# A kernel's input turned by products with diagonal matrices of reciprocal roots, instead of scaled and then turned

## The reference, cut to what matters

```python
def rms_norm(x, g):
    xf = x.astype(jnp.float32)
    y = xf * lax.rsqrt(jnp.mean(xf * xf, axis=-1, keepdims=True) + NORM_EPS)
    return (y * g.astype(jnp.float32)).astype(x.dtype)
...
    h = jnp.concatenate([meta, x], axis=1)
...
        u = rms_norm(h, mix_pre_g[l])
        proj = u @ w_in[l]
        hq, hf, hi, hg, cq, ckv, kpe, gates = jnp.split(proj, splits, axis=-1)
```

## Time and profile before

| | |
|---|---|
| median of 3 runs | 906.28 us |
| the profiled execution, its time | 904.64 us |
| its span | 902.8 us |
| TensorE busy with products | 881.4 us (98%) |
| TensorE busy with weight loads | 841.6 us (93%) |
| VectorE busy | 513.3 us (57%) |
| ScalarE busy | 473.4 us (52%) |
| GpSimd busy | 611.3 us (68%) |
| mean granted clock of TensorE | 0.996 |

### The profile page before, as it was taken

How to read it: one execution, slowest core, us unless ns; L and a number is a source line. 1 busy time by engine, 2 the same in 40 slices (tenths; PEclk the granted TensorE clock), 3 DMA queues, 4 the chain that set the end, 5 groups by cost and what they waited for, 6 DMA issues and landing times.

```text
span 902.8 us, 17105 instructions
## 1 busy us (share of the span) xinstructions
PE 881.4 (98%) x6837; PEld 841.6 (93%) x6837; DVE 513.3 (57%) x1108; ACT 473.4 (52%) x924; POOL 611.3 (68%) x349
## 2 busy tenths in 40 slices
PE   8999999999999999999999999999999999999996
PEld 7985999999998998999999999999988999999786
DVE  6404111599837857535431115878965668799464
ACT  5525755633346546544444444445657564456673
POOL 5702655655556987999998898776764877766153
PEclk9999999999999999999999999999999999999998
DMA  9623733343432564455655673654320627544201
GB/s 277 206 64 102 234 117 107 127 140 95 133 102 94 174 229 159 140 188 191 198 160 172 183 218 90 207 158 135 129 94 1 187 61 217 161 140 144 91 1 47
DMA packets 134334, 128.09 MB, mean 142 GB/s; under 512 B 6480, under 2 KB 131792, under 8 KB 134256
## 3 DMA queue, kind: packets, MB, share of 16 engines
q1 hardware_dynamic: 133776, 126.20, 44.8%
q10 hardware_dynamic: 480, 0.79, 0.3%
HBM read 125.80 MB, written 1.05 MB: 140 GB/s over the span
## 4 chain that ended last, share of the span: by engine, by line
PE 88%; DVE 6%; ACT 2%; issue 1%; DMA 1%; POOL 0%; POOLq 0%; DVEq 0%; ACTq 0%
PE PS L615 24%; PE PS L617 23%; PE PS L616 23%; PE PS L843 3%; PE PS L606 2%; PE PS L753 1%; PE PS L986 1%; DVE PS L2067 1%; PE PS L805 1%; PE PS L1046 1%; DMA ring<-in_w_in 1%; PE PS L801 1%; PE PS L802 1%; PE PS L1017 1%; ACT w_hi L1292 1%
## 5 line engine op out<-in xcount | busy, mean ns | idle before, releaser
L1160 POOL TENSOR_TENSOR w_lo<-ring,w_hi 128x1024 fp32r<-128x1024 f32 (+1 forms) x235 | 539.7, 2312 | 250.0 <-ACT w_hi L1292 239.4
L615 PE MATMUL PS<-x_hi,w_hi 128*128 128x256 f32 (+2 forms) x1560 | 458.3, 294 | 4.0 <-DVE x_lo L2021 0.9
L617 PE MATMUL PS<-x_hi,w_lo 128*128 128x256 f32 (+2 forms) x1560 | 443.9, 285 | 0.0
L616 PE MATMUL PS<-x_lo,w_hi 128*128 128x256 f32 (+2 forms) x1560 | 442.9, 284 | 0.0
L615 PEld LDWEIGHTS PS<-x_hi,w_hi 128*128 128x128 f32 (+1 forms) x1560 | 293.6, 188 | 8.9 <-issue 6.4
L616 PEld LDWEIGHTS PS<-x_lo,w_hi 128*128 128x128 f32 (+1 forms) x1560 | 293.1, 188 | 1.4 <-issue 0.2
L617 PEld LDWEIGHTS PS<-x_hi,w_lo 128*128 128x128 f32 (+1 forms) x1560 | 293.3, 188 | 0.0
L1292 ACT ACTIVATE w_hi<-ring 128x1024 fp32r<-128x1024 f32 (+2 forms) x233 | 235.5, 1014 | 78.7 <-PE PS L617 72.3
L2067 DVE SCALAR_TENSOR_TENSOR PS<-zoneA,cols,PS 128x256 f32<-128x256 f32 x240 | 98.6, 481 | 0.1
L1275 ACT ACTIVATE zoneA<-PS 128x272 f32<-128x272 f32 (+3 forms) x76 | 29.3, 386 | 107.8 <-PE PS L617 107.8
L1275 ACT ACTIVATE zoneB<-PS 128x256 f32<-128x256 f32 (+4 forms) x115 | 40.9, 378 | 70.7 <-DVE PS L2034 39.8
(11 more groups left out here) (300 smaller groups left out, 1196.0 us busy)
## 6 DMA issues: line engine op xcount, KB each, us to landing
ring<-in_w_in SPq DMA_DIRECT2D x58, 1024.0 KB, 5.4
ring<-in_w_ffn_in SPq DMA_DIRECT2D x22, 1024.0 KB, 5.1
ring<-in_w_out SPq DMA_DIRECT2D x12, 1024.0 KB, 5.0
ring<-in_w_ffn_out SPq DMA_DIRECT2D x16, 704.0 KB, 4.5
ring<-in_w_mla_o SPq DMA_DIRECT2D x4, 1024.0 KB, 5.0
ring<-in_w_hg_o SPq DMA_DIRECT2D x4, 1024.0 KB, 5.0
ring<-in_w_kv_b SPq DMA_DIRECT2D x2, 1024.0 KB, 5.5
ring<-in_w_q_b SPq DMA_DIRECT2D x2, 768.0 KB, 4.9
```

What stands on the lines that cost most here:

```text
L615: mm(out_, hi_w, hi_x, start=start, stop=False)
L616: mm(out_, hi_w, lo_x, start=False, stop=False)
L617: return mm(out_, lo_w, hi_x, start=False, stop=stop)
L1160: sub(lo_w, src, hi_w, ALU.subtract).then_inc(sem("w_lo"), 1)
```

## The change

ScalarE and VectorE no longer scale the input. VectorE multiplies the identity by the column of reciprocals and so makes three small diagonal matrices (16x16, 128x128, 128x128). TensorE no longer turns scaled rows: it multiplies the unscaled rows, as the stationary operand, by the diagonal as the moving one, which scales and turns in one ordinary float32 product. The diagonals come in the order meta rows, first tile, second tile, and TensorE waits for each once, in the first chunk. Waiting for the constants is added on VectorE. The results go to the same places of the same banks, and what follows is as before.

```diff
@@ -443,6 +443,7 @@
         x_nrm = zoneB[:, 4224:4224 + 3 * D].rearrange("p (t d) -> p t d", t=3)
+        x_diag = x_nrm[:, :, 0:P]
@@ -703,15 +704,13 @@
             pe.wait_ge(sem("const_in"), 16)
             for c in range(DC):
-                if c % 4 == 0:
-                    pe.wait_ge(sem(f"x_nrm{c // 4}"), 3)
                 if c >= 4:
                     pe.wait_ge(sem("lo_pre"), c - 3)
                 b = PS[:, 4 + c % 4, :]
-                nc.tensor.transpose(b[:, 0:META], x_nrm[0:META, 2, c * P:(c + 1) * P], ident[0:META, 0:META])
-                for t in range(2):
-                    last = nc.tensor.transpose(b[:, META + t * P:META + (t + 1) * P],
-                                               x_nrm[:, t, c * P:(c + 1) * P], ident)
+                for t, rows, x, at in ((2, META, m_tok[0:META, 0, :], 0), (0, P, x_tok[:, 0, :], META), (1, P, x_tok[:, 1, :], META + P)):
+                    if c == 0:
+                        pe.wait_ge(sem("x_diag"), (2, 3, 1)[t])
+                    last = mm(b[:, at:at + rows], x[:, c * P:(c + 1) * P], x_diag[0:rows, t, 0:rows], start=True, stop=True)
                 last.then_inc(sem("x_turned"), 1)
@@ -1328,10 +1327,6 @@
             af(x_rs, x_sums, ACT.Sqrt, scale=1.0 / D, bias=eps_rms).then_inc(sem("x_std"), 1)
-            act.wait_ge(sem("x_inv"), 1)
-            for half in range(2):
-                cols_ = slice(512 * half, 512 * half + 512)
-                af(x_nrm[:, 0, cols_], x_tok[:, 0, cols_], ACT.Copy, scale=x_rs[:, 0:1]).then_inc(sem(f"x_nrm{half}"), 1)
@@ -1743,11 +1738,10 @@
             dve.wait_ge(sem("m_in"), 16)
-            for half in range(2):
-                cols_ = slice(512 * half, 512 * half + 512)
-                for t, rows, x in ((1, P, x_tok[:, 1, cols_]), (2, META, m_tok[0:META, 0, cols_])):
-                    v.tensor_scalar(x_nrm[0:rows, t, cols_], x, x_rs[0:rows, t:t + 1], None, ALU.mult)\
-                        .then_inc(sem(f"x_nrm{half}"), 1)
+            dve.wait_ge(sem("const_in"), 16)
+            for t, rows in ((2, META), (0, P), (1, P)):
+                v.tensor_scalar(x_diag[0:rows, t, 0:rows], ident[0:rows, 0:rows], x_rs[0:rows, t:t + 1], None, ALU.mult)\
+                    .then_inc(sem("x_diag"), 1)
```

## The result

The kernel after takes 908.72 us, the median of 13 runs (907.61 to 912.11); the kernel before took 905.61 in the same comparison (13 runs, 904.5 to 908.34). The forecast was 907.6.

A forecast was written before the change was run, and what follows sets the result against it. TensorE was taken as the bound, busy 98% of the span: 2.32 us dearer products, less 0.67 for the earlier start and 0.35 for the stall, gave 1.30 later; 906.28 + 1.3 = 907.6 us, range 905.0 to 910.2.

The forecast's parts named there:

- Direction and place: TensorE's turning ahead of the first projection: dearer products make the kernel 1.3 us slower, passed on to the end.
- the mark: First weight load of the projections on TensorE: claimed to move from 14.03 to 15.33, between 14.85 and 17.25.
- The rate: TensorE's turning: a chunk claimed to cost 0.82 us, between 0.76 and 1.06, in place of 0.53.
- The start: TensorE's turning claimed to begin at 8.97, after the last warm-up record, in place of 9.64: 0.67 us earlier.
- The stall of 0.35 ahead of the fifth chunk: TensorE's wait before the fifth turned chunk: claimed to go, as that chunk would start at 12.25, after its release at 12.1.
- VectorE's freed time is worth nothing: VectorE before the first rounding: free at 9.22, but claimed to wait for first weights landing at 10.25, so no gain.
- The diagonals: Three small products on VectorE from 8.65: claimed about 0.2 us each, the third ready at 9.22, before TensorE asks.
- Absorption: Behind the turning: nothing claimed to absorb the shift; GpSimd would lose up to 0.9 us before its third difference.
- The granted clock: TensorE's clock in the turning: read as 1.00 (2.4 GHz) and left there.
- The first (no dearer in place): Rival for the turning: second records disappear in row-change gaps, chunk 0.53, first projection load at 14.03, time 906.3; chance 0.14.
- the third (four turns): Rival for the turning: a product costs four turns, chunk 1.35, 5.5 us later, time 911.8; chance 0.05.
- The second rival: First weights ready at 9.2, so roundings and x_lo move up 1.1 us; with cheap products, time 905.3; chance 0.05.

The follow-up runs named there:

- e3: The kernel after with the 16-row products of two chunks put together, so half as many row changes; 907.16 us, ratio 1.0011 to the kernel before.
- e4: The kernel before with 16-row turns of four and three chunks put together and seven banks for turned chunks; 905.03 us, ratio 0.9985.
- c1_before: The kernel before, unchanged, profiled a second time; span 903.4 us.
- e1: The kernel after, but TensorE turns unscaled rows with the identity; diagonals still made and waited for, no scaling done; 905.54 us, ratio 0.9999.
- e7: The kernel after with 4 unused products in place of 13 ahead of the turning; 913.94 us, ratio 1.0094.
- c2_after: The kernel after, unchanged, profiled a second time; span 907.1 us.

## Why the prediction was right, and where its sizes were off

**Direction and place: right; the size: less than half.** The time grew, within 0.5%, by TensorE's dearer products ahead of the first projection, passed on one to one (the table's last column). But 1.3 us were forecast and 3.1 measured. The 908.72 lies inside 905.0 to 910.2 because the range took in 1.06 us a chunk and the scatter of the runs, and not because the sum was good: the mark was forecast at 15.33, between 14.85 and 17.25, and stood at 16.78 in one profile and at 17.51, outside, in the other.

**The rate: a term too small.** The prediction took 0.82 us a chunk, between 0.76 and 1.06; it is 0.96. The pair was priced at 0.60 and is 0.64. The 16-row product was priced at 0.22, from products with 64-column weights, and is 0.32, the upper end. The term that was mis-sized is the change of rows. I had 0.15 us for the two changes of a chunk, from the pair of turns less 2 × 0.11; e3 measures 0.10 for the one and 0.19 for the other, and 6 × 0.11 + 0.29 gives 0.95. The 0.22 of the 16-row product left only its two records, and nothing for the change behind them. In the turns the missing part sat in the 16-row turn: its 0.16 is not one turn's work, since in e4 four of them stand some 0.06 apart ((0.32 − 0.14) / 3). And the earlier trace rows was no model for the 16-row product: it had half the columns to load, and its records come in pairs that start together (L1083 starts at 691.53 and 691.54, then at 691.59 and 691.60), so four of them took less than two of ours. Eight times 0.14 are 1.1 us of the 1.8 that the forecast was short.

**The start: a step that failed.** The prediction let the turning begin at 8.97, since the last unused product ended there in the one profile, and credited 0.67 us. The runs showed 9.29 and 10.02 for the same kernel, 9.66 in the mean, where the kernel before had 9.64 and 9.73. Nothing was won. In the kernel before the start was at whichever came last, the scalings or the unused products, and c1_before shows that it could already be the latter; when the scalings went, only the unused products were left. The end of these depends on when their rate doubles, and the one profile I had is the one with the earliest doubling of all (the section on the hardware below). For an execution like that one 8.97 may have been right; it was not for the others. In the kernel before, a late start hardly mattered, since the fifth chunk waits for x_lo anyway (marks 14.03 and 13.93). With 9.66 for 8.97 it is 0.7 us, and 1.3 + 1.1 + 0.7 = 3.1.

**The stall of 0.35 ahead of the fifth chunk: right**, it went; e1 shows it back when the rate is the old one.

**VectorE's freed time is worth nothing: right.** It waits for the first weights for 0.80 us after the diagonals, with the rounding at 10.19. In e1, where TensorE is cheap, the mark does not go below 13.83.

**The diagonals: right in effect.** The three take 0.61 from 8.78 on, where I had 0.57 from 8.65 on; without weight, since TensorE came later.

**Absorption: right.** GpSimd's third remainder slipped by 2.5 us (18.60, against 16.12 in the profile before, the third of the five from 11.06 on in the earlier trace rows), with a wait of 2.60 where up to 0.9 was foreseen, and TensorE has no wait for a remainder in the first 66 us of the kernel after.

**The granted clock: the reading was wrong.** I read 1.00 as the upper level. In the turning that was so, but the same column reads 1.00 in e7, where the same six records take 1.68. The column prints 1.00 for any stretch ahead of the trace's first clock record, so at the start of an execution it says nothing; the distance of the records does.

**The rivals.** The first (no dearer in place) and the third (four turns) are refuted by 0.96. The Trainium skill ("TensorE: Matmul & The Clock Gate", section "Terms") gives a factor of four for the turning mode in float32; the trace has 0.11 against 0.225 in streams, and 0.53 against 0.96 a chunk in place, so here it is about two, and the measurement decides. The second rival's condition wasn't met: in the kernel after, in e1 and in e3 VectorE waited for that transfer, 0.80 to 0.91 us, before the first rounding. It was not tried by moving the transfer; e4 shows that the floor lies one step further, at GpSimd's remainder.

## What to carry to other kernels

In this kernel an ordinary float32 product in place of a turn doubled TensorE's records, and such a change pays only if the engine has room there; here VectorE's and ScalarE's freed microseconds were worth nothing, since a transfer or TensorE itself was next. Before crediting an earlier start, ask what has been finishing just under the removed work, and look at it in more than one execution. Small products with other row counts are better put together: each change of rows cost 0.15 us between products and 0.12 between turns.

## What the runs showed of the hardware

**The rate of TensorE doubles at a moment that differs between executions.** In the kernel before, the weight loads of the unused products stood 0.43 us apart at first and 0.22 from about 4.9 us on; in c2_after they still stood 0.43 apart at 6.75 (1.2 GHz by the rate) and 0.21 after 7.3 (2.4 GHz). Weight loads of c2_after on either side, 0.34 and 0.19 us long, then of e7, 0.33 and 0.19:

```profile
6.33 0.34 PEld L704 LDWEIGHTS PS<-means 128*128 128x128 f32 x1
6.75 0.34 PEld L704 LDWEIGHTS PS<-means 128*128 128x128 f32 x1
7.33 0.19 PEld L704 LDWEIGHTS PS<-means 128*128 128x128 f32 x1
```

```profile
23.11 0.33 PEld L618 LDWEIGHTS PS<-x_hi,w_lo 128*128 128x128 f32 x1
...
23.53 0.19 PEld L617 LDWEIGHTS PS<-x_lo,w_hi 128*128 128x128 f32 x1
```

The granted clock of these stretches reads 1.00 throughout, but the packed traces date the rise: their first clock record, at full clock, stands at 4.79 us in the kernel before, 5.58 in the kernel after, 7.04 in c2_after and 23.46 in e7, each within 0.2 us of the place where the loads draw together. Over the nine profiles with thirteen unused products it lies between 4.79 and 7.39. With four unused products and 3.6 us of idleness behind them, the turning ran at the lower rate, 1.68 us a chunk for 0.96, to its end. The rise didn't come in these 13.14 us, of which TensorE was busy 13.11, but 1.5 us into the first projection. So nine of the thirteen products whose result nobody uses are worth 5.2 us to the kernel after (913.94 against 908.72, in two comparisons), although they also set its start.

**A change between 16-row and 128-row weights costs time each time**: in float32 products 0.15 us in the mean (0.10 towards 128 rows, 0.19 back; e3), in turns 0.12 (e4). The Trainium skill says that changing the tiling mode drains the engine (page "TensorEngine Tiling (Array Packing)", section "Tiling Modes"). The gaps fit that, if a change of rows counts as such a change; no run here shows that it does.

**A float32 product with 16 columns is no cheaper than one with 128.** A record takes 0.11 us in both: four 16-row records took 0.22 more in e3 (0.54) than two in the kernel after (0.32), the change behind them included in both. Both have weights of 128 columns, but these alone don't set the rate: the 16-row turns of e4 have the same weights and stand some 0.06 apart. What does isn't shown.
